# Attention stages: keys and values projected first, norms and rotation by column chunk, tile 0's output projection among the heads of tile 1

## The reference

```python
h = modulate(rms_norm(x, norm1_gain[i]), sh1, sc1)
hc = modulate(rms_norm(xc, norm1_gain[i]), csh1, csc1)
q, k, v = project_qkv(h, w_qkv[i], ...)       # y = h @ w_qkv; q, k normed by head and rotated
o = latent_global_attention(q, k, v, kc, vc)   # layer 0; layer 1: window mask and a sink
x = x + g1 * (o @ w_o[i])
h2 = modulate(rms_norm(x, norm2_gain[i]), sh2, sc2)
x = x + g2 * peer_ffn(h2, ...)                 # 8 x 16 experts per token, gathered by index
```

## Time and profile before

| what | us |
| --- | --- |
| median of 3 runs | 3406.18 (3397.04 to 3407.48) |
| the profiled execution, its own time | 3407.1 |
| its span, first to last instruction | 3405.3 |
| attention of the context, layer 0 | about 0 to 220 |
| attention of the latents, layer 0 | about 1480 to 1779 |
| attention of the last layer | about 2480 to 2698 |

### The profile page before, as it was taken

How to read it: one execution, slowest core, us unless ns; L and a number is a source line. 1 busy time by engine, 2 the same in 40 slices (tenths; PEclk the granted TensorE clock), 3 DMA queues, 4 the chain that set the end, 5 groups by cost and what they waited for, 6 DMA issues and landing times. The chain is left out here.

```text
span 3405.3 us, 25126 instructions
## 1 busy us (share of the span) xinstructions
PE 2522.5 (74%) x7884; PEld 1413.4 (42%) x7884; DVE 2155.7 (63%) x5140; ACT 475.2 (14%) x1396; POOL 1329.6 (39%) x1090
## 2 busy tenths in 40 slices
PE   5786196599996479972567888887766768888876
PEld 2353164467454348431444333333333433333432
DVE  1439745866566766557857667777526377777774
ACT  0210011100012100000111111111112111111111
POOL 0000023655463556545734445444300054454542
PEclk8888597599997589986678999999978889999998
DMA  6645164799995779987848999999850199999996
GB/s 253 251 179 220 60 236 164 267 326 385 379 339 189 247 276 393 378 306 272 290 148 361 418 418 419 419 422 421 354 196 25 44 415 419 418 419 422 421 421 283
DMA packets 248921, 1044.63 MB, mean 307 GB/s; under 512 B 20518, under 2 KB 53398, under 8 KB 176852
## 3 DMA queue, kind: packets, MB, share of 16 engines
q0 software_dynamic: 147456, 805.37, 59.7%
q1 hardware_dynamic: 93584, 222.23, 17.6%
q10 hardware_dynamic: 7748, 15.43, 1.3%
HBM read 1040.23 MB, written 2.72 MB: 306 GB/s over the span
## 5 line engine op out<-in xcount | busy, mean ns | idle before, releaser
L1173 POOL DMA_INDIRECT sb_beside_slots<-in_peer_uv,sb_beside_chosen x512 | 599.5, 1171 | 409.8 <-DVE sb_xc L1165 261.9
L1146 DVE SCALAR_TENSOR_TENSOR sb_beside_slots<-sb_beside_slots,sb_beside_H 128x1024 f32<-128x1024 f32 x256 | 312.8, 1223 | 261.6 <-DMA sb_beside_slots<-in_peer_uv,sb_beside_chosen 260.0
L1165 DVE SCALAR_TENSOR_TENSOR sb_xc<-sb_beside_slots,sb_beside_small,sb_xc 128x1024 f32<-128x1024 f32 x254 | 325.5, 1282 | 3.9 <-DMA sb_beside_slots<-in_peer_uv,sb_beside_chosen 2.0
L174 PE MATMUL psum<-sb_f_arena,sb_f_ring 128*128 128x256 f32 (+1 forms) x1344 | 297.5, 385 | 8.6 <-issue 8.6
L174 PEld LDWEIGHTS psum<-sb_f_arena,sb_f_ring 128*128 128x128 f32 (+1 forms) x1344 | 252.7, 188 | 53.0 <-issue 10.6
L174 PE MATMUL psum<-sb_f_ring,sb_f_arena 128*128 128x512 f32 (+2 forms) x448 | 195.8, 599 | 5.5 <-DVE sb_f_arena L1769 5.5
L1079 PE MATMUL psum<-sb_latents_ring,sb_latents_scores 128*128 128x512 f32 x304 | 147.4, 636 | 50.1 <-ACT sb_latents_scores L1037 50.1
L1079 PE MATMUL psum<-sb_last_ring,sb_last_scores 128*128 128x512 f32 x276 | 138.9, 653 | 51.2 <-ACT sb_last_scores L1037 51.2
L2036 PE MATMUL psum<-sb_f_ring,sb_f_arena 128*128 128x512 f32 x384 | 165.4, 592 | 0.0
L1079 PE MATMUL psum<-sb_beside_slots,sb_latents_scores 128*128 128x512 f32 x288 | 139.5, 630 | 32.3 <-ACT sb_latents_scores L1037 32.3
L935 POOL DMA_INDIRECT sb_latents_ring<-in_peer_uv,sb_latents_scores x76 | 92.2, 1213 | 132.4 <-PE psum L1079 90.8
(11 more groups left out here) (503 smaller groups left out, 4778.0 us busy)
## 6 DMA issues: line engine op xcount, KB each, us to landing
sb_f_ring<-in_w_ff SPq DMA_DIRECT2D x32, 2048.0 KB, 12.4
sb_context_ring<-in_ada_w SPq DMA_DIRECT2D x24, 2048.0 KB, 9.7
sb_f_ring<-in_w_in SPq DMA_DIRECT2D x8, 2048.0 KB, 14.0
sb_f_ring<-in_w_in SPq DMA_DIRECT2D x6, 1904.0 KB, 12.3
sb_context_ring<-in_peer_w_q SPq DMA_DIRECT2D x8, 1024.0 KB, 8.0
sb_beside_slots<-in_peer_uv,sb_beside_chosen POOLq DMA_INDIRECT x512, 6.4
sb_f_ring<-in_w_out SPq DMA_DIRECT2D x4, 2048.0 KB, 8.0
sb_latents_ring<-in_peer_w_q SPq DMA_DIRECT2D x8, 1024.0 KB, 25.1
```

The source lines that it names most:

```text
L174: last = e.matmul(out, a, b, start=(i == 0), stop=(i == len(terms) - 1))
L1146: e.scalar_tensor_tensor(out=self.u_slot[s % 4], in0=self.u_slot[s % 4], scalar=1.0, in1=self.H[:, s // (PH * TOPK), :], op0=ALU.mult, op1 ...
L1165: e.scalar_tensor_tensor(out=acc, in0=row, scalar=wn, in1=acc, op0=ALU.mult, op1=ALU.add).then_inc(self.added, 1)
L1173: return e.indirect_dma_start(out=to, out_offset=None, in_=self.table, in_offset=bass.IndirectOffsetOnAxis(ap=at, axis=0), element_offset= ...
```

## The change

The diff touches `attention` alone, for all three stages.

- Keys and values (chunk 2) are loaded and projected first, then chunk 0 and chunk 1.
- The norms and the rotation are cut by chunk: `squared(c)` needs only the groups of chunk c, `finished(c)` only its power. One instruction now covers all tiles of a chunk, and one rotation instruction both halves of the rotated columns. The 22 steps of `more(22)` are put between these parts as 6, 6, 4 and 6. TensorE's transposes wait for their own chunk.
- For the latents and the last layer, tile 0's oT, both its wo chunks and its h2T are put into the head loop at turns 9, 10, 12 and 16 (`among`); VectorE's part stands at turns 11, 13, 14 and 15. After the loop only tile 1's remain.
- The rows 3 and 4 of the second modulation are loaded after the first norm and scaled ahead of the head loop; the row 5 is loaded late, as before.
- GpSimd has six powers in place of four, each with a mark of its own.

```diff
-    qkv = [(c, g) for c in range(3) for g in (0, 2) if g in (q_tiles if c < 2 else h_tiles)]
+    qkv = [(c, g) for c in (2, 0, 1) for g in (0, 2) if g in (q_tiles if c < 2 else h_tiles)]
...
+    turned_pairs = (4, 0, 1, 2, 3)
+    order += [("QT", hp) for hp in turned_pairs]
+    g0, g1 = q_tiles
+    tail = lambda g: [("oT", g), ("wo", g, 0), ("wo", g, 1), ("h2T", g)]
+    among = {} if context else dict(zip((9, 10, 12, 16), tail(g0)))
...
+        order += [among[i]] if i in among else []
...
-    prod = [work[:, 1024 * j:1024 * (j + 1)].rearrange("p (t n) -> p t n", t=2) for j in range(2)]
+    prod = [gains[:, 0, 512 * j:512 * (j + 1)] for j in range(2)]
...
-    plan += [(chunk(wqkv, c), ("qkv",) + [x for x in qkv if x[0] == c][-1]) for c in range(3)]
+    plan += [(chunk(wqkv, c), ("qkv",) + [x for x in qkv if x[0] == c][-1]) for c in (2, 0, 1)]
...
+            e.wait_ge(h_ready, nh)
+            for j in (1, 0):
+                e.dma_start(mod[:, j, :], rows[0:1, 3 + j, :].to_broadcast([P, D])).then_inc(mods_in[2], 16)
...
+            if not context and i == 9:
+                transposed(("oT", g0))
+            if not context and i == 13:
+                square_of(0)
...
+            transposed(("h2T", g0))
+            transposed(("oT", g1))
+            square_of(1)
+            e.dma_start(mod[:, 2, :], rows[0:1, 5, :].to_broadcast([P, D])).then_inc(mods_in[1], 16)
+            transposed(("h2T", g1))
...
-        more(22)
-        for c, g in qkv:
-            e.wait_ge(*st.emptied(("qkv", c, g)))
-        parts = [(0, H2, q_tiles, 0, rs[:, 0:8 * nq]), (H2, KV2, h_tiles, 1, rs[:, 32:32 + 2 * nh])]
-        scr = QT[:, :, :].rearrange("p h n -> p (h n)")
-        for h0, n, tiles, gain, r in parts:
-            for j, g in enumerate(tiles):
-                y = Y[:, g - n0, h0 * HD2:(h0 + n) * HD2]
-                spot = scr[:, 2048 * gain + n * HD2 * (j % 2):2048 * gain + n * HD2 * (j % 2 + 1)]
-                e.tensor_tensor(spot, y, y, ALU.mult).then_inc(*own.up())
-                e.wait_ge(*own.now)
-                summed = e.tensor_reduce(r[:, j * n:(j + 1) * n], spot.rearrange("p (h d) -> p h d", d=HD2), AX, ALU.add).then_inc(*own.up())
-            e.wait_ge(*own.now)
-            rms_rows(e, r, r, HD2).then_inc(var, 1)
...
+        def squared(c):
+            h0, n, tiles, gain, r = parts[c]
+            for x in qkv:
+                if x[0] == c:
+                    e.wait_ge(*st.emptied(("qkv",) + x))
+            spot = flat(QT[:, h0:h0 + n, :], "p h n -> p (h n)")[:, 0:len(tiles) * n * HD2]
+            e.tensor_tensor(spot.rearrange("p (g n) -> p g n", g=len(tiles)), y_all(h0, n, tiles), y_all(h0, n, tiles), ALU.mult).then_inc(*own.up())
+            e.wait_ge(*own.now)
+            e.tensor_reduce(r, spot.rearrange("p (g d) -> p g d", d=HD2), AX, ALU.add).then_inc(*own.up())
+            e.wait_ge(*own.now)
+            up = HD2 if gain == 0 else 1
+            e.tensor_scalar(r, r, up / HD2, EPS * up, ALU.mult, ALU.add).then_inc(var, 1)
...
+            e.tensor_tensor(y, y, wide(r.rearrange("p (g h) -> p g h", h=n), [P, len(tiles), n, HD2], 3), ALU.mult).then_inc(*own.up())
+            e.wait_ge(*own.now)
+            e.wait_ge(late, 48 if context else 64)
+            done = e.tensor_tensor(y, y, wide(qkg[:, gain, :], [P, len(tiles), n, HD2], 1, 1), ALU.mult)
...
+                y1, y2 = yr[:, :, :, 0, :], yr[:, :, :, 1, :]
+                tab = lambda name: wide(L(name)[:, g * 64:(g + 1) * 64].rearrange("p (a d) -> p a d", a=2), [P, n, 2, 32], 1)
+                ta = [work[:, 1024 * g + 256 * j:1024 * g + 256 * j + 64 * n].rearrange("p (h a d) -> p h a d", h=n, a=2) for j in range(4)]
+                e.tensor_tensor(ta[0], y1, tab("cos2"), ALU.mult).then_inc(*own.up())
...
+        squared(2)
+        more(6)
+        squared(0)
+        finished(2, 2)
+        more(4)
+        finished(0, 3)
+        squared(1)
+        more(6)
+        finished(1, 4)
...
+        def projected(g, c):
+            to = prod[x_step.n % 2]
+            e.wait_ge(*st.computed(("wo", g, c)))
+            if x_step.n >= 2:
+                e.wait_ge(x_ready, x_step.n - 1)
+            e.tensor_tensor(to, st.pair(("wo", g, c))[:, 0, :], mod[:, 2, c * 512:(c + 1) * 512], ALU.mult).then_inc(*st.empties(("wo", g, c)))
+            e.wait_ge(*st.emptied(("wo", g, c)))
+            xv = xs[g][:, c * 512:(c + 1) * 512]
+            e.tensor_tensor(xv, xv, to, ALU.add).then_inc(*x_step.up())
...
+        def second_norm(j):
+            g = q_tiles[j]
+            e.wait_ge(rstd, 5 + j)
+            e.scalar_tensor_tensor(out=rows2(g), in0=xs[g], scalar=rs2[:, j:j + 1], in1=mod[:, mod_row(v, 1), :], op0=ALU.mult, op1=ALU.mult).then_inc(*own.up())
+            e.wait_ge(*own.now)
+            e.tensor_tensor(rows2(g), rows2(g), mod[:, mod_row(v, 0), :], ALU.add).then_inc(h_ready, 1)
+
+        if not context:
+            e.wait_ge(mods_in[2], 32)
+            scaled(1, 16, [0])
...
+            if i in (11, 13):
+                projected(g0, (i - 11) // 2)
+            if i == 14:
+                variance(0)
+            if i == 15:
+                second_norm(0)
...
-        normed(q_tiles, rows2, ss2, rs2, nh + 2, 4, [("mB", c) for c in range(6, 10)] if context else [])
+                more(3)
+                projected(g1, c)
+            variance(1)
+            second_norm(1)
+            e.wait_ge(mods_in[1], 32)
...
-        for turn, (r, n) in enumerate(((rs1, nh), (rs, 8 * nq), (rs[:, 32:40], 2 * nh), (rs2, nq))):
+        for turn, (r, n) in enumerate(((rs1, nh), (rs[:, 32:40], 2 * nh), (rs[:, 0:8], 4 * nq), (rs[:, 8:16], 4 * nq), (rs2[:, 0:1], 1), (rs2[:, 1:2], 1))):
...
+            if group[0] == "oT":
+                e.wait_ge(*st.emptied(("o", 8 * n + 7)))
+                transposes(group)
+            elif group[0] == "wo":
+                e.wait_ge(*st.emptied(("oT", g)))
+                e.wait_ge(*landed(("wo", g1, group[2])))
+                project(group, weights_of(("wo", g1, group[2])), (g,))
+            else:
+                e.wait_ge(h_ready, nh + n + 1)
+                transposes(group, rows2)
...
-        e.wait_ge(y_ready, n_y)
-        for hp in range(5):
+        for hp in turned_pairs:
             g_ = ("QT", hp)
+            e.wait_ge(y_ready, 1 if hp == 4 else 2 + hp // 2)
...
+            if i in among:
+                tail_group(among[i])
...
+            for group in tail(g1):
+                tail_group(group)
```

149 lines of the change are left out of this document (71 added, 78 removed).

## The result

The changed kernel takes 3379.48 us, median of 5 runs (3377.94 to 3382.38), against 3407.48 for five runs of the kernel before on the same chip. The ratio is 0.9924 with a 95% interval of 0.9911 to 0.9936: by the ratio 26 us (22 to 30) are gained, by the medians 28, where the prediction has 44. The sign was right; the size was not. The median lies 1.5 us inside the upper end of the range, and that is no credit to the sum, whose centre is 17 us away and whose own range ended at 3375.

What follows compares the result with a forecast made beforehand. It took the last layer's front and both tails as TensorE-VectorE chains, the latents' heads as VectorE-bound. Its terms summed to -43.7 us from 3407.1, giving 3363.4, less 0.9: 3362.5 us, range 3349 to 3381.

Steps and rivals of the forecast that it cites:

- Term 4: Latents, ahead of the heads: norms between steps let gathers load, GpSimd's powers give most back; -1 us.
- Rival R1: Latents' front: GpSimd's three waits each cost their 8.0 us with nothing filling; +7 to +10, total 3373; chance 0.12.
- Term 2: Last layer, heads: tile 0's wo blocks, oT, chunk reading and second norm lengthen the loop; +18.9 us.
- term 1: Last layer, ahead of the heads: keys first and norms by chunk bring the scores earlier; -17.6 us.
- term 3: Last layer, last scaling to the experts' queries: one tile's projection and norm less, rows early; -24 us.
- Term 5: Latents, heads: work added to VectorE, which bounds there, and two stalls by wo blocks; +5.5 us.
- Rival R2: Latents' heads: the wo blocks run at 1.2 GHz; +10 us, total 3373; chance 0.10.
- Term 6: Latents, tail from last scaling to queries: shortened as in the last layer, 49.4 to 25.9; -23.5 us.
- Term 7: Context: same instructions cut by tile, waiting for half the columns and for tile 0's own power; -2 us.
- R3: Latents' front bound by bytes alone: -15.5 us there, total 3349; chance 0.08.
- R4: Work moved into loops gives all of it back; only the last layer's norms remain, -17.6 us, total 3388; chance 0.06.
- R5: Last layer's heads: TensorE waits, its clock falls to 1.2 GHz; +63 us, total 3407 or slower; chance 0.04.

Runs made afterwards that it cites:

- e8: Changed kernel with all 22 steps ahead of the norms, gates as in the changed kernel: 3370.0 us, ratio 0.9903 to the kernel before.
- e3: Changed kernel with GpSimd allowed to issue more steps ahead of its three powers of queries and keys (gates opened): 3366.6 us, ratio 0.9875 to the kernel before.
- e12: Changed kernel, gates closed, with modulation rows 3 and 4 loaded behind the projection's last copy: 3372.1 us, ratio 0.9906 to the kernel before.
- e9: Changed kernel with gates open, tile 0's tail among the heads in the latents alone, 92 unused transposes before chunk 1's rotation in the last layer: 3353.0 us.
- e4: Changed kernel with VectorE reading tile 0's two projected chunks one turn earlier (turns 10 and 12): 3383.5 us, ratio 0.9931 to the kernel before.
- e7: Changed kernel with gates open, tile 0's tail behind the loops, rows 3 and 4 loaded and scaled behind the w_o projection: 3377.3 us.
- e1: Changed kernel with tile 0's oT, wo and second norm back behind the head loop in latents and last layer: 3373.4 us, ratio 0.9915 to the kernel before.
- e2: Changed kernel with tile 0's tail among the heads in the last layer alone: 3384.6 us, ratio 0.9931 to the kernel before.

## Why the prediction was off

**Term 4 failed (-1 recorded, +8.4 measured), and it is over half of the miss.** Two steps of it were wrong.

The first is the overlap of norm work with gathers: "VectorE fills about 2.5 with a ready step and some 4 with norm work at two of them, give back most of it." I priced the wait for rows behind a power. I didn't price that norm work ahead of a power keeps the gate shut: GpSimd issued nothing for 9.96 us before the first power (VectorE was waiting for the projected keys, DMA was still full) and for 9.90 before the third (VectorE was at chunk 0's norm and chunk 1's squares, DMA moved 2 GB/s). e8 shows that against uncut steps the cut costs 4.5 us, and e3 that opening the gates gives 10.0 back.

The second is that the modulation rows "are hidden by GpSimd's waits in mine". They are not behind those waits but ahead of them, among the first weights: TensorE waits 10.07 us for these in place of 6.95, and e12, which moves their load behind the projection, reaches the first maximum 4.2 us sooner. The wait for the first weights is 8.7 to 11.9 us in the nine traces with early rows and 5.8 to 7.0 in the five without. I had worked out 2.6 us for the rows (1 MB at 402 GB/s) if they were not hidden. The Trainium skill (*DMA: Bandwidth & Descriptors*, section *Issuing engines are not separate DMA queues*) says that transfers of all queues run on the same 16 engines and interleave. The trace agrees, since a load from ScalarE's queue held up weights from SyncE's; and the weights came 3.1 (against before) to 3.7 us (against e12) later, more than the bytes' 2.6.

The two make up the term: 4.5 for the cut (e8) and 3.9 for the rest between e8 and the kernel before, which e12's 4.2 for the rows covers. Rival R1, given 0.12, had +7 to +10 for GpSimd's waits alone. That 8.4 falls in it is luck: without the rows the closed gates leave the term at +4.2 (e12), below R1's range.

**Term 2 (+18.9 recorded, +24.5 measured)** was above its own upper bound of 23. The two blocks cost 14.1, as priced. Missing was the clock: of the 24 transposes that stood ahead of the scores 8 remained, TensorE stood 10.25 us before them, and the loop began at 0.50, +2.5 us (e9). The reading of the chunks was booked at 1.7 through VectorE's line; the price is that scores wait for the PSUM pair, 2.08 twice, 2.5 of which e4 takes away. A further 1.7 is in this trace alone: after the second wait the clock dipped (0.58 over 4 us) and scores took 2.08; in five other kernels with this loop the heads take 67.5 or 67.6. What is left of the 24.5, some 2.0 by subtraction, is for oT and the second norm, booked at 3.3 net. The Trainium skill (*TensorE: Matmul & The Clock Gate*, Part 1) has the lower level for an engine that was not kept busy. The start of the loop agrees with it, with 10.25 us idle ahead of 8 transposes; the dip doesn't decide it, because the same two waits of 2.08 left the level alone in the five others.

**Terms 1 and 3 held**: -17.6 for -17.6, -24.2 for -24. That term 1 fits to the tenth is in part luck: the same front takes 71.7 to 73.7 in other traces. Its working has 12.4 us for chunk 1 where its own steps add up to 11.5; the sum doesn't use the 12.4. In term 3 the early rows with their DMA issues are worth 4.7 (e7), where 4.0 and 1.3 were booked.

**Term 5 (+5.5, measured +8.7)**: the blocks are 4 to 5.5 of it (e1 and e2 without them take 116.4 and 115.7; nine kernels with blocks, read as in the changed kernel, take 119.5 to 122.0, 120.5 in the mean). The other 2.5 to 3 us against before appear without blocks too, but not in e7 (114.1); I can't tell them from scatter. **Rival R2** is refuted: both blocks ran at clock 1.00, in 7.05 and 7.03 us. I had also put a price of 13.9 per block to the rule of the Trainium skill (*TensorE: Matmul & The Clock Gate*, Part 1). But the rule, as I told it, is for an engine that isn't kept busy, and inside a block TensorE has no gap (6.80 of 6.80 us): the loop's mean clock of 0.67 said nothing of a dense block.

**Term 6 (-23.5, measured -20.8)**: tile 1's projection takes 16.19 us where 14.00 do in the last layer, since it begins with 4 us at 0.50. The kernel before didn't have that cost: its projection of both tiles began at 1.00 and took 27.70. Nor is it tied to the blocks in the loop, because with both tiles behind the loop it took 29.71 (e1), 27.63 (e2) and 29.76 (e7). What decides the level there stays open.

**Term 7 (-2, measured -7.0)**: the tail of the context is 4.6 shorter (52.3 to 47.7; 46.2 to 47.9 in the other traces). The two reasons that I gave came as booked: TensorE's wait ahead of tile 0's h2T went from 8.53 to 6.59 us. I had left out that tile 0's projection no longer waits for tile 1's oT (some 1.4), and 1.4 us in the projection itself (29.69 to 28.30; 27.63 and 28.88 in two others). The other 2.4 us of -7.0 lie ahead of its heads and are scatter: the first maximum stands between 141.6 and 147.5 in the traces with this same code, and at 146.7 before. The +3.1 of the experts, whose code is the same, I leave open: the stretch takes 733.5 to 738.2 us in the twelve other traces and 733.0 in the only one of the kernel before.

**R3 and R4** mark the ends: opened gates reach about 119 from hT and 114.7 with the rows out of the way, 6 us below before, so the norms do hide if GpSimd is let go, though not down to R3's lower end; and in the last layer R4 held: a tail moved into a loop that TensorE fills came back in full (heads and tail 93.0 against 88.6 without it). **R5** did not occur: the clock over the last layer's heads was 0.91.

## What to carry to other kernels

An engine whose program holds both gathers and small powers makes each wait of the one a gap of the other. When work is cut and interleaved, move the point up to which the gathers may run ahead too; else the cut costs more than it hides (4.5 us here, against 5.5 gained with the gates open). Work moved among a loop pays where the loop's engine has waits (latents: 5 us for 15) and not where it is the bound (last layer: 20 for 16). A load taken off a tail is put in front of something else; look who else loads at its new place.

## What the runs showed of the hardware

TensorE's granted clock counted where I had not looked. Removing transposes that seemed pure cost (24 became 8) let the last layer's loop start at 0.50 instead of 1.00; 92 unused ones in the idle stretch ahead of it gave 2.5 us back in the heads, while 48 that ended 4.95 us early gave nothing. And two loads of a modulation row to all partitions, 512 KB each, among 402 GB/s of other traffic delayed the weights by 3.1 to 3.7 us, where their bytes alone are 2.6.
